# The norms of a two-model chain on one core: tensor arithmetic from GpSimd to VectorE and ScalarE

## The reference

```python
def layer_norm(x, g, b):
    mu = jnp.mean(x32, axis=-1, keepdims=True)
    var = jnp.mean(jnp.square(x32 - mu), axis=-1, keepdims=True)
    return (x32 - mu) * lax.rsqrt(var + LN_EPS) * g + b
...
    for i in range(DEPTH):
        h = x * (1.0 + sc_m) + sh_m
        y = even_mixer(...) if i % 2 == 0 else odd_mixer(...)
        x = layer_norm(ALPHA * x + (1.0 + g_m) * y, ln_mix_g[i], ln_mix_b[i])
        h = x * (1.0 + sc_f) + sh_f
        y = swiglu(h, w_gate[i], w_up[i], w_down[i])
        x = layer_norm(ALPHA * x + (1.0 + g_f) * y, ln_ffn_g[i], ln_ffn_b[i])
...
def rmsnorm(x, w):
    return x * lax.rsqrt(jnp.mean(x * x, axis=-1, keepdims=True) + EPS) * w
```

## Time and profile before

| | |
|---|---|
| median of 3 runs | 1178.07 us (1175.09 to 1179.08) |
| the profiled execution | 1179.2 us, its span 1177.9 us |
| busy: PE, DVE, ACT, POOL | 1134.8, 846.7, 628.0, 77.1 us |
| mean granted clock of TensorE | 0.987 |
| HBM | 229.56 MB read, 196 GB/s over the span |
| chain that ended last | PE 84%, DVE 10%, ACT 2%, issue 2%, DMA 1%, POOL 0% |

### The profile page before, as it was taken

The page is one execution under the profiler, slowest core; times in us unless marked ns, Lnnn a source line. Parts: engine busy times, 40 slices in busy tenths (PEclk is TensorE's granted clock), DMA queues, the critical chain, the costliest instruction groups (busy, mean ns, idle before and its releaser), DMA issues.

```text
span 1177.9 us, 23803 instructions
## 1 busy us (share of the span) xinstructions
PE 1134.8 (96%) x9940; PEld 1069.9 (91%) x9940; DVE 846.7 (72%) x1437; ACT 628.0 (53%) x1075; POOL 77.1 (7%) x101
## 2 busy tenths in 40 slices
PE   5999898999999999999999999999999999999998
PEld 3888578999998899898999999999999999999987
DVE  5679679897995788797557569858746667776743
ACT  3358437545443677666545445744554556555542
POOL 3000012000000200021000003500000001000000
PEclk8999899999999899999999999999999999999999
DMA  9953856898998634645665562653245554556550
GB/s 327 350 198 109 291 173 213 285 309 266 338 308 282 215 115 144 208 133 179 211 193 175 187 212 72 215 181 110 86 134 188 168 183 157 179 181 214 179 179 36
DMA packets 194683, 232.15 MB, mean 197 GB/s; under 512 B 4083, under 2 KB 169555, under 8 KB 194576
## 3 DMA queue, kind: packets, MB, share of 16 engines
q1 hardware_dynamic: 193984, 230.32, 59.1%
q0 software_dynamic: 592, 0.31, 0.2%
HBM read 229.56 MB, written 1.05 MB: 196 GB/s over the span
## 4 chain that ended last, share of the span: by engine, by line
PE 84%; DVE 10%; ACT 2%; issue 2%; DMA 1%; POOL 0%; SPq 0%; DVEq 0%; ACTq 0%
PE ps L154 83%; DVE wlo L187 2%; PE ps L157 2%; DVE hL L196 1%; DVE T L187 1%; ACT whi L166 1%; DVE first L187 1%; DVE LT L196 1%; DMA raw<-in_w_in_dram 1%; DVE LT L187 0%; DVE T L196 0%; DMA RV<-in_b_mod_dram 0%; DMA MW<-in_w_mod_dram 0%; DVE Fg L196 0%; DVE MR L196 0%
## 5 line engine op out<-in xcount | busy, mean ns | idle before, releaser
L187 DVE TENSOR_TENSOR wlo<-raw,whi 128x1024 fp32r<-128x1024 f32 (+1 forms) x346 | 408.4, 1202 | 162.6 <-ACT whi L166 161.0
L154 PE MATMUL ps<-hH,whi 128*128 128x256 f32 (+3 forms) x1792 | 518.4, 289 | 3.7 <-DVE hL L187 3.1
L154 PE MATMUL ps<-hH,wlo 128*128 128x256 f32 (+3 forms) x1792 | 507.5, 283 | 7.6 <-DVE wlo L187 7.6
L154 PE MATMUL ps<-hL,whi 128*128 128x256 f32 (+3 forms) x1792 | 507.2, 283 | 0.0
L166 ACT ACTIVATE whi<-raw 128x1024 fp32r<-128x1024 f32 (+1 forms) x346 | 349.2, 1032 | 198.2 <-PE ps L154 142.9
L154 PEld LDWEIGHTS ps<-hH,whi 128*128 128x128 f32 x1792 | 340.3, 190 | 15.2 <-issue 11.1
L154 PEld LDWEIGHTS ps<-hH,wlo 128*128 128x128 f32 x1792 | 340.7, 190 | 8.8 <-DVE wlo L187 8.8
L154 PEld LDWEIGHTS ps<-hL,whi 128*128 128x128 f32 x1792 | 341.0, 190 | 0.3
L154 PE MATMUL ps<-uL,whi 128*128 128x256 f32 x352 | 99.2, 282 | 0.0
L154 PE MATMUL ps<-uH,whi 128*128 128x256 f32 x352 | 99.0, 281 | 0.0
L154 PE MATMUL ps<-uH,wlo 128*128 128x256 f32 x352 | 98.4, 279 | 0.0
(11 more groups left out here) (312 smaller groups left out, 1622.0 us busy)
## 6 DMA issues: line engine op xcount, KB each, us to landing
MW<-in_w_mod_dram SPq DMA_DIRECT2D x47, 1024.0 KB, 6.5
raw<-in_w_up_dram SPq DMA_DIRECT2D x44, 1024.0 KB, 5.5
raw<-in_w_in_dram SPq DMA_DIRECT2D x36, 1024.0 KB, 5.1
raw<-in_w_down_dram SPq DMA_DIRECT2D x27, 1024.0 KB, 5.3
raw<-in_w_gate_dram SPq DMA_DIRECT2D x22, 1024.0 KB, 7.3
raw<-in_w_in_odd_dram SPq DMA_DIRECT2D x12, 1024.0 KB, 6.2
raw<-in_w_in_even_dram SPq DMA_DIRECT2D x8, 1024.0 KB, 6.8
raw<-in_w_down_dram SPq DMA_DIRECT2D x8, 768.0 KB, 6.7
```

Of the source, the lines that this page charges most:

```text
L154: return self.queued(self.e.matmul(out, lhsT, rhs, start=start, stop=stop, skip_group_check=True, **kw), length if pos is None else max(le ...
L187: return self.queued(self.e.tensor_tensor(out, a, b, op), 0.07 + cols(out) / self.RATE)
```

## The change

The sum of squares goes to VectorE, in `layer_norm` (`add_square`, placed one iteration later, and two adds behind `residual(6)`) and in `rms_norm`. In the h loop, `z` is now T times rstd in place by tensor_tensor; ScalarE makes zh with scale and bias, waits for itself and copies it to hH; hL is a plain difference and comes two blocks later instead of one. The new x then needs ScalarE alone, one op per 0.6 us of TensorE's planned time. In norm 4 VectorE does all products with rstd. `gated` waits for the last hL and no longer for the last XA.

```diff
+    def add_square(i):
+        return dve.wait_ge(*squared[i]).settle().tt(sqa, sqa, sq[i], ALU.add).inc()
+
     for j in (0, 2, 4):
...
         square(j + 1)
-        for i in (j, j + 1):
-            if i == 0:
-                pool.wait_ge(*squared[0])
-            else:
-                total = pool.wait_ge(*squared[i]).settle().tt(sqa, sqa, sq[i], ALU.add).inc()
+        if j == 2:
+            dve.wait_ge(*squared[0])
+        for i in (j - 2, j - 1):
+            if i > 0:
+                add_square(i)
...
     residual(6)
     square(6)
+    add_square(4)
+    total = add_square(5)
...
-        total = pool.wait_ge(*squared[6]).settle().tt(sqa, sqa, sq[6], ALU.add).inc()
         yield due(part)
     alone = where[6][0] != where[7][0]
     pe.wait_ge(*part).mm(mean, ones[:, 0, :], acc, alone, False)
+    if alone:
+        yield due(squared[6])
+        total = add_square(6)
...
-        for i in range(KD + 1):
+        for i in range(KD + 2):
             if i < KD:
                 dve.wait_ge(*e[i])
                 if i >= 4:
-                    dve.wait_ge(*hi[i - 4])
-                z[i] = dve.stt(zh[i % 4], T(i), hs[:, i:i + 1], rstd, ALU.mult, ALU.mult).inc()
+                    act.wait_ge(*k.h_low[i - 4])
+                z[i] = dve.tt(T(i), T(i), rstd, ALU.mult).inc()
...
-                hi[i] = act.wait_ge(*z[i]).act(m.hH[:, i, TOK], zh[i % 4], ACT.Identity, bias=hb[:, i:i + 1]).inc()
+                act.wait_ge(*z[i]).act(zh[i % 4], T(i), ACT.Identity, scale=hs[:, i:i + 1], bias=hb[:, i:i + 1])
+                hi[i] = act.settle().act(m.hH[:, i, TOK], zh[i % 4], ACT.Copy).inc()
...
-            if i > 0:
-                n = i - 1
-                k.h_low[n] = dve.wait_ge(*hi[n]).stt(m.hL[:, n, TOK], zh[n % 4], hb[:, n:n + 1], m.hH[:, n, TOK].bitcast(F32), ALU.add, ALU.subtract).inc()
+            if i > 1:
+                n = i - 2
+                k.h_low[n] = dve.wait_ge(*hi[n]).tt(m.hL[:, n, TOK], zh[n % 4], m.hH[:, n, TOK].bitcast(F32), ALU.subtract).inc()
                 yield dve.clock - 0.5
-        pool.wait_ge(*z[KD - 1])
+        k.hold = False
+        for j in range(KD):
+            yield k.pe.clock + 0.6
+            new[j] = act.act(X(j), T(j), ACT.Identity, scale=ag[:, j:j + 1], bias=ab[:, j:j + 1]).inc()
     else:
         less_mean(4, 5, 6, 7)
-        pool.wait_ge(*e[KD - 1]).wait_ge(*rstd_done)
-    k.hold = False
-    for i in range(0, KD, 2):
-        if to is not None:
+        k.hold = False
+        dve.wait_ge(*e[KD - 1])
+        for i in range(0, KD, 2):
             for j in (i, i + 1):
-                t = pool.tt(T(j), T(j), rstd, ALU.mult).inc()
-                yield due(t)
-                new[j] = act.wait_ge(*t).act(X(j), T(j), ACT.Identity, scale=ag[:, j:j + 1], bias=ab[:, j:j + 1]).inc()
-        else:
-            t = pool.tt(T(i), T(i), rstd, ALU.mult).inc()
-            dve.wait_ge(*e[i + 1]).tt(T(i + 1), T(i + 1), rstd, ALU.mult)
-            yield due(t) - 0.3
-            dve.wait_ge(*t).settle()
+                dve.tt(T(j), T(j), rstd, ALU.mult)
+            dve.settle()
             for j in (i, i + 1):
                 new[j] = dve.ts(X(j), T(j), g[:, j:j + 1], ALU.mult, b[:, j:j + 1], ALU.add).inc()
+            yield dve.clock - 0.3
...
-    while not k.normed or k.raw_done is None:
+    while k.raw_done is None:
         yield None
...
-        for mark in (*k.normed, k.raw_done):
-            act.wait_ge(*mark)
+        act.wait_ge(*k.h_low[KD - 1]).wait_ge(*k.raw_done)
...
-            square = pool.wait_ge(*square).tt(before, before, sq, ALU.add).inc()
+            square = dve.wait_ge(*square).tt(before, before, sq, ALU.add).inc()
```

More of the change, by code:

```diff
@@ L1486, in layer_norm @@
 def layer_norm(k, where, l, chunk, g, b, to=None, x=None, freed=None, early=True):
-    pe, act, dve, pool, m = k.pe, k.act, k.dve, k.pool, k.m
+    pe, act, dve, m = k.pe, k.act, k.dve, k.m
     LT = [m.LT[:, 256 * i:256 * i + 256] for i in range(9)]
```

## The result

The changed kernel takes 1182.76 us (median of 8 runs, 1181.51 to 1186.61), the kernel before 1178.17 beside it (8 runs). The ratio is 1.0047, with a 95% interval of 1.0028 to 1.0065: slower, where I had forecast 1171.5. The profiled execution took 1182.3 us, its span 1180.7.

A forecast was written before the change was run, and what follows sets the result against it. TensorE was taken as the bound, stalled by VectorE's late wlo while VectorE and GpSimd exclude one another. Terms -3.7 - 3.4 + 0.8 + 0.5 - 0.7 = -6.5 us gave 1171.5 us, range 1166.5 to 1181.

The forecast's parts named there:

- Step (1): Norms 1 and 3: products with 1/std leave GpSimd, "first" x4 takes 1.43 us, wlo follows 2.19 us sooner in each.
- Step (3): Products making XA: ScalarE ops before and after, now spread one per 0.6 us; claimed to cost nothing.
- step (2): h loop: doubled ScalarE pass adds 0.53 us latency; last hL 0.36 us later, between 1.0 earlier and 1.5 later.
- the cover: Norm 1's h loop: last hL out 2.2 us before TensorE needs it; 1.8 us was to stay.
- Case (d): Rival: conversions between doubled ScalarE passes make the last hL 2.4 us late; slower, 1180 to 1185, say 1182; chance 0.16.
- Case (c): Rival: queues behind norm 1 are planned anew, TensorE meets another late weight, gain given back; about 1178, chance 0.14.
- Step (4): Squares' adds on VectorE delay the mean's matmul: +0.4 us (0 to 0.9) in norms 1 and 3, nothing in 2 and 4.
- Step (5): Norm 2: the two ScalarE passes lengthen TensorE's wait for the first h: +0.5 us (0 to 0.9).
- Step (6): Norm 4 and first RMS norm: TensorE's 1.3 us of waits for GpSimd's adds halve: -0.7 us (0 to -1.3).
- my reading of the earlier trace as a point between 1.17 and 1.73 us: TensorE's clock falls after stalls above this point; stalls left of 1.1 us would save 1.7 us in norms 1 and 3.

The follow-up runs named there:

- the old h loop: Changed kernel with the h loop and SiLU wait of the kernel before, each XA queued when its product is due: 1172.33 us, ratio 0.9948.
- the three orders: Before, changed, and changed with old h loop, each planned with the planner's lag of a mark at 0.13, 0.135 and 0.14: 1162.0 to 1182.8 us.
- 0.135: Planner's lag of a mark 0.135 instead of 0.13 us, same instructions: before 1169.3, changed 1173.5, changed with old h loop 1168.6 us.
- the x products alone: Kernel before with only the T x rstd products for the new x moved from GpSimd to VectorE: 1172.28 us, ratio 0.9947.
- the 1191.0 us: Changed kernel with the old h loop, XA's products on VectorE and each XA queued straight behind its product, new SiLU wait: 1191.0 us, ratio 1.0117.
- four orders: Kernel before at lag 0.13, 0.135, 0.14: 1178.2, 1169.3, 1170.7 us; with TensorE's planned clock 0.3 us forward near 375 us: 1187.66 us.
- the other good parts: Kernel before with the new x's products and norm 4's products on VectorE, squares and h loop as before: 1169.19 us, ratio 0.9922.
- lag 0.14: Planner's lag of a mark 0.14 instead of 0.13 us, same instructions: before 1170.7, changed 1169.8, changed with old h loop 1162.0 us.

## Why the prediction was wrong

**What held.** Step (1): "first" x4 took 1.43 us in every kernel without GpSimd's products. From the products of the raw values to the group behind s = 1 (182 to 209 us of the kernel before) the old h loop with this step gains 2.8, 1.6 and 3.1 us on before in the three orders (1.85 + 1.7 was forecast for norm 1; at 0.135 before's own stall there is 1.97 us and costs no clock), and the x products alone gain 3.7 behind norm 3. Step (3), as a price of ScalarE's work, held in the version with the x products; it is free only if XA never waits at the head of ScalarE's queue (the 1191.0 us). In step (2) the sizes of the operations were right (pair 1.04 us), and so was the last hL: it was not late.

**The step that failed is (2).** I named the danger, "behind that wait on ACT stand the conversions to whi", and then measured the cover on hL alone, 2.2 us. The late item was not hL but the second halves of s = 1's own weights. I also worked out the next wlo as "202.19 - 2.19 + 0.36" as if the queue in front of it stayed the same; two low halves that had been done before "first" moved behind it, so TensorE met its wait inside the group, not at its end. Priced at 0.36 us for the hL, the doubled pass, with the SiLU wait that goes with it, cost 4.9 to 10.4 us. Of the 10.4, about 2.5 are the pass itself in an unchanged order. The rest was not taken apart: it holds the order that the pass's modelled cost brings about, the SiLU wait, and the stall near 484, which only this one order has. Of the 11 us between 1171.5 and 1182.8, about 6 lie behind norm 1 (3.1 less was forecast, 2.9 more came), which is mostly this step; about 7 lie near 484 and were in no term of the sum; the later norms give some back. (A small slip in the cover: 95 intervals between 188.89 and 200.36 are 1.45 us a block, not 1.42, so the last h was needed near 199.0. It changes nothing.)

**Rivals.** Case (d) had the sign, and 1182 beside 1182.8, but not the mechanism: it needed the last hL 2.4 us late, and it came 0.5 us early. Case (c) had the re-planning, but only as giving a gain back. It can cost and it can gain: the kernel before spans 1169.3 to 1187.7 us over four orders. That spread was in no term, and it is wider than my whole range.

**Step (4)** is of uncertain size: 0.8 was forecast; the squares cost 1.8 alone and 3.1 beside the other good parts (1172.3 less 1169.2), but the changed kernel is 3.1 us faster with them than without (1182.8 against 1185.9), each in its own order. What the trace does show is a longer way to the mean's matmul. VectorE between the last wlo and the mean's matmul, changed kernel:

```profile
169.74 0.47 DVE L196 SCALAR_TENSOR_TENSOR T<-ps,MOD,XA 128x256 f32<-128x256 f32 x1
170.32 0.95 DVE L187 TENSOR_TENSOR LT<-LT 128x256 f32<-128x256 f32 x2
171.31 0.42 DVE L187 TENSOR_TENSOR LT<-LT,T 128x256 f32<-128x256 f32 x1
```

From residual 6 to the matmul it is 171.88 - 169.74 = 2.14 us, in the kernel before 171.80 - 170.72 = 1.08 (its residual 6 is at 170.72): 1.06 more, a little over the bound of 0.9, in part because the two dependent adds start 0.53 us apart and not 0.46. The larger miss is what I took for cover: TensorE had come to the matmul 1.80 us early and had nothing else in its queue. The Trainium skill ("VectorE: DVE Perf Modes", The DRAIN you can't avoid) has a semaphore between two operations, measured there on copies, at no extra cost; the 0.53 us of these adds beside the 0.335 of independent ones don't agree with it.

**Step (5)**: TensorE's wait for norm 2's first h grew from 0.59 to 0.89 us, 0.3 for my 0.5. The trace of before had a slow stretch of the clock there and the changed one hasn't, which is why the offset falls by 2.5 us, to +1.6, in this norm. That is no gain of the change.

**Step (6)** looks undersized the other way: 2.1 us of gain alone, over the bound of 1.3, which its interval doesn't exclude; in the traces it is 2.8. The waits that I counted account for the 1.4 us at 722 us; another 1.4 came between 722 and 800, in the new order behind norm 4, where I had not looked.

**What stays open.** Why VectorE comes late to 484 us in some orders was not settled: moving TensorE's transposes didn't help, and the rows show a wait of VectorE for TensorE of 3 us and then four low halves that were queued together. Nor was the SiLU wait tried apart: the one version with the old h loop and the new SiLU wait (1191.0 us) also queued XA otherwise. And three orders are few: that the changed h loop costs in any order is likely, not proven.

## What to carry to other kernels

When an operation is added to an engine that also prepares the weights, follow every queued item behind it to its reader, not only the operation's own result: an item that slips past a block of other work pays for that whole block. Where a planner orders the queues by modelled costs, plan both kernels in a few orders before believing a difference of under 1%. And of one change, time the parts: here, in the planner's own order, two of four were worth 9 us together, and one cost as much.

## What the runs showed of the hardware

A stall's length didn't decide alone whether TensorE's clock falls. The changed kernel stood 1.80 us at 171.88 and stayed up:

```profile
172.00:180.00 8.00, 7.05 (x55) 4.57 (x56) 5.75 (x22) 5.73 (x13) 0.00 (x0) 1.00 0.42 135
```

while the squares alone, with 1.87 us at the same matmul, were followed by 6.8 us at 0.50 (above). In the kernel before at lag 0.135, a stall of 2.76 us behind norm 3, the length of the earlier trace rows, cost no clock either:

```profile
528.37 0.39 PE L154 MATMUL ps<-hH,wlo 128*128 128x256 f32 x1 [2.76 <-DVE wlo L187]
```

```profile
528.00:538.00 10.00, 9.47 (x78) 9.27 (x79) 8.54 (x11) 7.50 (x11) 0.00 (x0) 1.00 0.67 208
```

At lag 0.14 TensorE stood 1.45 us before the mean's matmul in the changed kernel and in the one with the old h loop alike; then the clock was at its lower level in the changed kernel (first window) and up in the other (second):

```profile
171.00:174.00 3.00, 3.00 (x14) 3.00 (x15) 3.00 (x8) 3.00 (x6) 0.00 (x0) 0.51 1.04 384
```

```profile
171.00:174.00 3.00, 3.00 (x27) 3.00 (x27) 3.00 (x8) 3.00 (x6) 0.00 (x0) 1.00 1.04 369
```

So my reading of the earlier trace rows as a point between 1.17 and 1.73 us was no rule. In these traces a stall between 1.45 and 2.82 us cost nothing more, or 1.7 us (3.5 us at the lower level), or 3.4 (6.8 us, the squares alone). So one trace against another can differ by a few us through the clock alone; the kernel before itself ran between 1175.1 and 1181.1 us.
